# Streamed weights through three buffers, an earlier norm for tile 1, and a ring of gathered rows at a multiple of 8192 bytes

## What is computed

```python
x = x + jnp.concatenate([y_s5, y_m2], axis=-1) @ w_out           # "x_mid" in the kernel
h = rmsnorm(x, norm_ffn_w)
q = (h @ w_q).reshape(T, 8, 2, 128)
s = jnp.einsum('thid,hikd->thik', q, sub_keys)                   # scores
sv, si = lax.top_k(s, 16)                                        # twice, then 16 of 16 x 16
g = jax.nn.softmax(cv, axis=-1)
act = jax.nn.gelu(jnp.einsum('thkd,td->thk', u_tab[idx], h))
x = x + jnp.einsum('thk,thkd->td', g * act, v_tab[idx])          # 128 rows of u and v for each token
y = rmsnorm(x, final_norm_w)
```

## Time and profile before

| what | us |
|---|---|
| median of 3 runs | 4046.57 |
| lowest and highest of them | 4043.29, 4048.2 |
| the profiled execution | 4042.5 |
| its span, first to last instruction | 4040.7 |
| first gather, from the start of the span | 1122.5 |

### The profile page before, as it was taken

The page is one execution under the profiler, slowest core; times in us unless marked ns, Lnnn a source line. Parts: engine busy times, 40 slices in busy tenths (PEclk is TensorE's granted clock), DMA queues, the critical chain, the costliest instruction groups (busy, mean ns, idle before and its releaser), DMA issues.

```text
span 4040.7 us, 47356 instructions
## 1 busy us (share of the span) xinstructions
PE 2634.4 (65%) x16198; PEld 1280.3 (32%) x16198; DVE 2380.2 (59%) x4877; ACT 1190.8 (29%) x2963; POOL 1365.4 (34%) x1291
## 2 busy tenths in 40 slices
PE   7999844978886689764654564564474465455444
PEld 4556733544642233241421231141141141122110
DVE  2355094764556555467577477467567657747744
ACT  2011011114154222233333333333332333333332
POOL 4000010320033444444444444444444444434442
PEclk9999977989998799875755665675585576576555
DMA  3322132457588999998999999999999999999998
GB/s 119 75 71 67 70 40 88 136 178 256 199 314 328 400 421 422 417 417 365 420 421 421 416 421 420 403 420 420 401 420 421 403 418 421 417 404 421 420 413 352
DMA packets 279656, 1318.52 MB, mean 326 GB/s; under 512 B 51632, under 2 KB 111152, under 8 KB 137136
## 3 DMA queue, kind: packets, MB, share of 16 engines
q0 software_dynamic: 156672, 1140.92, 68.4%
q1 hardware_dynamic: 122704, 174.13, 13.4%
HBM read 1266.08 MB, written 46.51 MB: 325 GB/s over the span
## 4 chain that ended last, share of the span: by engine, by line
DMA 45%; issue 12%; PE 9%; DVE 6%; ACT 5%; POOL 1%; POOLq 0%; SPq 0%; DVEq 0%; ACTq 0%
DMA pe_ring<-in_uv,pe_index_now 45%; PE pe_acc L2053 4%; DVE pe_ring L1848 3%; PE pe_ps_q L1916 2%; PE pe_ps_q L1977 2%; ACT pe_mark L1597 1%; ACT L1597 1%; ACT pe_weight L1599 1%; PE pe_ps_t L2046 1%; DMA scratch_s_t<-pe_shared 1%; DVE pe_shared L1655 1%; POOL pe_ring L1475 1%; ACT L1576 0%; PE pe_ps_q L2016 0%; ACT L1559 0%
## 5 line engine op out<-in xcount | busy, mean ns | idle before, releaser
L1848 DVE CUSTOM_DVE_ANT_0 pe_ring<-pe_ring,pe_h_rep 128x1024 f32<-128x1024 f32 x1088 | 1329.2, 1225 | 978.6 <-DMA pe_ring<-in_uv,pe_index_now 927.8
L1475 POOL DMA_INDIRECT pe_ring<-in_uv,pe_index_now x1088 | 1229.0, 1130 | 1575.2 <-PE pe_acc L2053 1407.2
L2053 PE MATMUL pe_acc<-pe_ring,pe_weight 128*32 128x256 f32 x8704 | 980.1, 539 | 1139.4 <-ACT pe_weight L1599 1137.0
L1597 ACT ACTIVATE pe_mark<-pe_same,pe_dot 128x32 f32<-128x32 f32 x1088 | 349.3, 321 | 1782.9 <-DVE pe_dot L1848 1780.3
L2053 PEld LDWEIGHTS pe_acc<-pe_ring,pe_weight 128*32 128x32 f32 x8704 | 205.8, 128 | 1893.5 <-ACT pe_weight L1599 1806.2
L1599 ACT ACTIVATE pe_weight<-pe_mark,pe_gate_now 128x32 f32<-128x32 f32 x1088 | 349.7, 321 | 35.2
L558 PE MATMUL pj_bank<-pj_x_t,pj_w_buf 128*128 128x512 f32 (+1 forms) x960 | 316.0, 491 | 2.7 <-DVE pj_x_t L419 2.7
L2016 PE MATMUL pe_ps_q<-pe_shared,early_space 128*128 128x128 f32 x1792 | 262.5, 307 | 0.0
L2016 PEld LDWEIGHTS pe_ps_q<-pe_shared,early_space 128*128 128x128 f32 x1792 | 239.3, 215 | 47.6 <-issue 47.6
L1977 PE MATMUL pe_ps_q<-early_space,pe_shared 128*128 128x512 f32 x448 | 223.9, 623 | 1.2 <-DVE pe_shared L1655 1.2
L558 PEld LDWEIGHTS pj_bank<-pj_x_t,pj_w_buf 128*128 128x128 f32 x960 | 158.5, 192 | 155.6 <-issue 153.9
(11 more groups left out here) (317 smaller groups left out, 2697.1 us busy)
## 6 DMA issues: line engine op xcount, KB each, us to landing
pe_ring<-in_uv,pe_index_now POOLq DMA_INDIRECT x1088, 16.0
pe_ring<-in_w_out SPq DMA_DIRECT2D x8, 2048.0 KB, 9.0
pe_ring<-in_w_q SPq DMA_DIRECT2D x8, 2048.0 KB, 11.2
pj_w_buf<-in_w_in SPq DMA_DIRECT2D x13, 1024.0 KB, 6.2
early_space<-in_w_out SPq DMA_DIRECT2D x2, 4096.0 KB, 15.9
early_space<-in_w_q SPq DMA_DIRECT2D x8, 1024.0 KB, 47.7
scratch_xbc<-pj_z_out SPq DMA_DIRECT2D x12, 552.0 KB, 4.4
m2s_xbc<-scratch_xbc SPq DMA_DIRECT2D x8, 768.0 KB, 5.1
```

Of the source, the lines that this page charges most:

```text
L1475: nc.gpsimd.indirect_dma_start(out=ring[:, p, :], out_offset=None, in_=D["uv"], in_offset=bass.IndirectOffsetOnAxis(ap=row, axis=0)).then_ ...
L1597: A(mark[:, p % 2, :], eye, ACT.Gelu_apprx_tanh, scale=dot[:, p:p + 1]).then_inc(mark_ready, 1)
L1848: V.tensor_tensor_reduce(out=ring[:, p, 0:D_MODEL], in0=ring[:, p, 0:D_MODEL], in1=h_rep[:, g % 2, :], scale=1.0, scalar=0.0, op0=ALU.mult ...
L2053: last = T.matmul(acc[j * PER:(j + 1) * PER, g % 2, 0:COLS], lhs(j), src[:, j * COLS:(j + 1) * COLS], start=first, stop=final)
```

## The change

1. The pieces go through three buffers: slots 6 and 7, 2 and 3, 4 and 5. `piece_load(i)` waits for piece i - 3. SP issues pieces 0 to 2 at the start, piece 3 ahead of the S5 stores, 4 and 5 between and behind the last gate stores.
2. To make room, the sets of tiles 0 and 1 shrink to one slot each (slots 1 and 0): `res_of` takes the place of `ym_of`, whose transposes have been made by then, and is loaded later; tile 1's S5 tile goes into `h_rep[:, 1]`, once the gate store that reads this buffer has landed.
3. POOL's waits follow the new places: gather 1 (before: 2) waits for `score_moved`; gathers 2, 4 and 6 wait for 6, 7 and 8 query products.
4. `mix(1, X_MID)` stands behind step `SUMS + 2` of `route(0)` instead of `SUMS + 4`, and `route(1, NORM)` behind `SUMS + 4` instead of `SUMS + 6`.
5. Small tensors are allocated ahead of the ring and large ones behind it, so that the ring starts at byte 90,112 of each partition (before: 142,912). With it all tensors allocated behind `pick` move.

```diff
         pick = sb("pick", [P, GROUPS, GROUPS, PER])
+        final_w = sb("final_w", [P, COLS])
+        gate_now = sb("gate_now", [P, SLOTS])
+        mark = sb("mark", [P, 2, PER])
+        count16 = sb("count16", [P, TOPK])
+        norm_w = sb("norm_w", [P, 2 * KT])
+        ring = sb("ring", [P, RING, 2 * D_MODEL])
         ffn_w = sb("ffn_w", [P, D_MODEL])
...
-        piece = [space[:, 8192:12288], space[:, 12288:16384]]
+        piece = [space[:, 4096 * i:4096 * i + 4096] for i in (3, 1, 2)]
...
-        sets = [space[:, 4096:8192], space[:, 0:4096], shared[:, 0:4096], shared[:, 4096:8192]]
+        sets = [space[:, 2048:4096], space[:, 0:2048], shared[:, 0:4096], shared[:, 4096:8192]]
...
-        res_of = lambda m: sets[MIX_SET[m]][:, 1024:2048] if m < EARLY else sets[MIX_SET[m]][:, 3072:4096]
-        m2_of = lambda m: sets[MIX_SET[m]][:, 3072:4096].rearrange("p (c n) -> p c n", c=KT)
+        m2_flat = lambda m: sets[MIX_SET[m]][:, 1024:2048] if m < EARLY else sets[MIX_SET[m]][:, 3072:4096]
+        m2_of = lambda m: m2_flat(m).rearrange("p (c n) -> p c n", c=KT)
+        res_of = lambda m: ym_of(m) if m < EARLY else m2_flat(m)
...
+        s5_tile = lambda m: (h_rep[:, 1, :] if m < EARLY else sets[MIX_SET[m]][:, 2048:3072]).rearrange("p (c n) -> p c n", c=KT)
...
             def piece_load(i):
-                if i >= 2:
-                    sp.wait_ge(*piece_done(i - 2))
+                if i >= 3:
+                    sp.wait_ge(*piece_done(i - 3))
...
-            for i in range(2):
+            for i in range(3):
                 piece_load(i)
-            for m in range(EARLY):
-                sp.dma_start(res_of(m), D["x_all"][rows(m), :]).then_inc(res_in[m], 16)
...
             for m in range(2, TILES):
                 gate_load(m)
+            for m in range(EARLY):
+                sp.wait_ge(m2_turned, m + 1)
+                sp.dma_start(res_of(m), D["x_all"][rows(m), :]).then_inc(res_in[m], 16)
+            piece_load(3)
             sp.wait_ge(s5_ready, KT)
             for b in BLOCK_0:
                 s5_store(0, b, lambda m: s5_1_out if m == 1 else s5_0_out)
-            piece_load(2)
             gate_store(TILES - 2)
-            piece_load(3)
+            piece_load(4)
             gate_store(TILES - 1)
+            piece_load(5)
             sp.wait_ge(s5_1_out, 32)
+            sp.wait_ge(gate_out[1], 16 * (TILES // 2 - 1))
             sp.dma_start(s5_tile(1), D["s5_t"][1]).then_inc(s5_in[1], 16)
-            for i in range(4, 6):
-                piece_load(i)
...
-                    if front and n == 2:
+                    if front and n == 1:
                         pool.wait_ge(score_moved, 1)
-                    if front and n == 4:
-                        pool.wait_ge(q_made, EARLY * UNITS)
+                    if front and n in (2, 4, 6):
+                        pool.wait_ge(q_made, EARLY * UNITS - 3 + n // 2)
...
                 route(0, g, False, 0)
+                if g == SUMS + 2:
+                    mix(1, X_MID)
                 if g == SUMS + 4:
-                    mix(1, X_MID)
-                if g == SUMS + 6:
                     route(1, NORM, True, 1)
```

More of the change, by code:

```diff
@@ L1161, in route_and_experts @@
         pick = sb("pick", [P, GROUPS, GROUPS, PER])
+        final_w = sb("final_w", [P, COLS])
[4 more added lines that the diff above has]
+        ring = sb("ring", [P, RING, 2 * D_MODEL])
         ffn_w = sb("ffn_w", [P, D_MODEL])
-        final_w = sb("final_w", [P, COLS])
-        count16 = sb("count16", [P, TOPK])
         eps = sb("eps", [P, 1])
@@ L1179, in route_and_experts @@
         work_b = shared[:, 6144:8192]
-        norm_w = sb("norm_w", [P, 2 * KT])
         gate_sq = sb("gate_sq", [P, TILES, 2])
@@ L1200, in route_and_experts @@
         gate = e
-        ring = sb("ring", [P, RING, 2 * D_MODEL])
-        mark = sb("mark", [P, 2, PER])
         weight = sb("weight", [P, RING, PER])
@@ L1207, in route_and_experts @@
         h_rep = sb("h_rep", [P, 2, D_MODEL])
-        gate_now = sb("gate_now", [P, SLOTS])
         index_now = sb("index_now", [P, 2, HALF], I32)
@@ L1245, in s5_of @@
         def s5_of(m, c):
-            return s5_out(0, c)[:, first(0):first(0) + P] if m == 0 else sets[MIX_SET[m]][:, 2048 + c * P:2048 + (c + 1) * P]
-        s5_tile = lambda m: sets[MIX_SET[m]][:, 2048:3072].rearrange("p (c n) -> p c n", c=KT)
+            return s5_out(0, c)[:, first(0):first(0) + P] if m == 0 else s5_tile(m)[:, c, :]
+        s5_tile = lambda m: (h_rep[:, 1, :] if m < EARLY else sets[MIX_SET[m]][:, 2048:3072]).rearrange("p (c n) -> p c n", c=KT)
         acc = ctx.enter_context(nc.psum_tensor("pe_acc", [P, 2, 512], F32))
@@ L1269, in route_and_experts @@
         set_3_free = sem("set_3_free")
-        piece_in = [sem("piece_in_even"), sem("piece_in_odd")]
+        piece_in = [sem(f"piece_in{i}") for i in range(3)]
         consts_in, x_in, eps_set, made, summed, root, h_ready = (sem(n) for n in (
@@ L1316, in piece_load @@
             def piece_load(i):
-                if i >= 2:
-                    sp.wait_ge(*piece_done(i - 2))
+                if i >= 3:
+                    sp.wait_ge(*piece_done(i - 3))
                 kind, at = PIECES[i]
                 if kind == "out":
-                    sp.dma_start(out_piece[i % 2], D["w_out"][:, at:at + 4]).then_inc(piece_in[i % 2], 16)
+                    sp.dma_start(out_piece[i % 3], D["w_out"][:, at:at + 4]).then_inc(piece_in[i % 3], 16)
                 else:
-                    sp.dma_start(q_piece[i % 2], D["w_q"][:, :, at * UNIT * P:(at + 1) * UNIT * P]).then_inc(piece_in[i % 2], 16)
+                    sp.dma_start(q_piece[i % 3], D["w_q"][:, :, at * UNIT * P:(at + 1) * UNIT * P]).then_inc(piece_in[i % 3], 16)
             def s5_store(n, b, sem_of):
@@ L1950, in early_out @@
                         pe.wait_ge(s5_ready, KT)
-                pe.wait_ge(piece_in[i % 2], 16 * (i // 2 + 1))
+                pe.wait_ge(piece_in[i % 3], 16 * (i // 3 + 1))
                 for c in range(4 * j % KT, 4 * j % KT + 4):
                     for b in range(2):
-                        last = T.matmul(acc[:, b, :], m2_of(m)[:, c, :] if j < 2 else s5_of(m, c), out_piece[i % 2][:, c % 4, b * 512:b * 512 + 512],
+                        last = T.matmul(acc[:, b, :], m2_of(m)[:, c, :] if j < 2 else s5_of(m, c), out_piece[i % 3][:, c % 4, b * 512:b * 512 + 512],
                                         start=j == 0 and c == 0, stop=j == 3 and c == KT - 1)
@@ L2012, in route @@
                                 i = Q_PIECE[early] + n
-                                pe.wait_ge(piece_in[i % 2], 16 * (i // 2 + 1))
+                                pe.wait_ge(piece_in[i % 3], 16 * (i // 3 + 1))
                         for c in range(KT):
-                            w = w_q[:, c, j * P:(j + 1) * P] if early is None or early == 2 else q_piece[(Q_PIECE[early] + n) % 2][:, c, j % UNIT * P:(j % UNIT + 1) * P]
+                            w = w_q[:, c, j * P:(j + 1) * P] if early is None or early == 2 else q_piece[(Q_PIECE[early] + n) % 3][:, c, j % UNIT * P:(j % UNIT + 1) * P]
                             last = T.matmul(ps_q[:, n % 2, j % UNIT, :], w, h_t[:, c, :],
```

## The result

| | before | after |
|---|---|---|
| median of the runs, us | 4047.39 (4043.29 to 4051.75) | 3988.12 (3983.34 to 3988.76) |
| profiled execution, and its span, us | 4042.5, 4040.7 | 3987.48, 3985.7 |
| the stage's first load to the first gather, us | 894.82 to 1122.47: 227.65 | 898.42 to 1101.29: 202.87 |
| first gather to the end of the span, us | 2918.2 | 2884.4 |
| one tile of 128 gathers, tiles 3 to 6, us | 327.3 to 327.6 | 322.6 to 323.1 |

The ratio is 0.9849, with a 95% interval from 0.983 to 0.9869. A fourth run of the kernel after took 5732.11 us: it is in the median of 3988.12 us, but not in the range and the ratio, and the median of the other three is 3987.48. The third and the fourth row of the table say where the difference lies.

A forecast was written before the change was run, and what follows sets the result against it. PE, waiting for weight loads, was taken to bound the stage ahead of the first gather; 12.77 + 1.11 + 4.33 + 1.70 + 4.70 = 24.6 us off the profiled 4042.5 gave 4017.9, as median 4022.0, range 3996 to 4034.

The forecast's parts named there:

- The first late load: Front, PE's wait for weight piece 2: 11.23 us of wait and 1.54 us of slow clock go, together 12.77.
- The cover of piece 3: Front: piece 3 lands at about 972 us, PE wants it at 975.8; cover 4 us, beyond that each us costs one.
- The other loads: Front, later weight pieces: w_q waits go for 4.33 us, 2.22 shrinks for 1.11, tile 1's wait and clock give 4.70.
- Tile 1's norm: Front, VectorE: with the norm two steps sooner, it ends near 1073.4 instead of 1075.1 us; 1.70 us gained.
- What was costed at nothing in the front: Moved residual loads, SyncE's new waits and the second gather's wait for ScalarE's copy on POOL: hidden, priced at zero.
- The ring's address: Gathered rows landing in the ring, moved from 64 above a multiple of 256 onto one: 0 to 3 ns cheaper, taken as zero.
- the far bound: Upper end of the gain per ring row from the new address: 3 ns.
- rival 1: Gather loop: the ring's new place makes rows 3 ns cheaper, 23 us more gained, 3999 us; chance 0.13.
- everything behind the first gather only moves: Gather loop: same stretch from first gather to end within 8 us, so the front's gain arrives at the end unchanged.
- The 3 ns between the two 4 KB loads: Loads of x_all (aligned, 159.5 ns a row) and x (224 above a multiple, 162.5 ns), used to bound the ring's price.
- The two loads by which the prediction bounded the price: Loads of x_all and x, 4 KB rows at 159.5 and 162.5 ns, bounding an aligned row's gain at 0 to 3 ns.

The follow-up runs named there:

- ring_m64: Changed kernel with one 64-byte tensor moved from ahead of the ring to behind it, ring 192 above a multiple of 256; 4022.47 us.
- ring_m128: Changed kernel with two 64-byte tensors behind the ring instead of ahead, ring 128 above a multiple of 256; 4019.97 us.
- ring_m256: Changed kernel with one 256-byte tensor moved behind the ring, which starts at 89,856, a multiple of 256 but not of 512; 3988.39 us.
- ring_p32: Changed kernel with one 32-byte tensor moved ahead of the ring, ring 32 above a multiple of 256; 4025.23 us.
- ring_back: Changed kernel with the allocation order of the kernel before, ring again 64 above a multiple of 256; 4026.64 us, ratio 0.9942 to the kernel before.
- ring_only: Kernel before with only the allocation order of the changed kernel, ring at byte 90,112; 4013.55 us, ratio 0.992 to the kernel before.
- piece4_first: Changed kernel with the load of piece 4 issued ahead of the six S5 stores; 3988.54 us, ratio 0.9852 to the kernel before.

## Why the prediction was wrong

**The first late load: right.** 11.23 us and 1.54 us were to go. The pair of pieces 2 and 3 starts as the pair before it ends and takes 13.90: 12.77 us. The cover of piece 3 held.

**The other loads: right for w_q, one wait missed.** All brackets of 1.70, 1.01, 1.62 and 3.10 us are gone, and 2.22 became 1.11. What I did not look at is piece 4. I took two pieces of PE's time, 14 us or more, as the cover of every later load, and for that the load has to start as soon as its buffer is free. Piece 4 stands behind the S5 stores on SyncE, and these got slower. Before, PE waited 1.56 us at this place for VectorE:

```profile
997.09 7.10 PE L1954 MATMUL pe_acc<-pe_ring 128*128 128x512 f32 x16 [1.56 <-DVE pe_x L1655]
```

Now it waits 2.30 us for the DMA, and the 16 products behind took 8.72 us instead of 7.10. Cost: 0.74 + 1.62 = 2.4 us. In ring_m64 and ring_m128 the wait is 2.48 us and the products take 7.10 or 7.11, and in ring_m256 and ring_p32 PE waits 1.56 us for VectorE again, so the cost is anything from nothing to 2.4 us. The clock of the kernel after at this place:

```profile
988.30:995.10 6.80, 6.80 (x13) 2.96 (x14) 1.59 (x3) 0.52 (x3) 0.00 (x0) 0.77 1.06 414
```

0.77 is a mixture of the two levels, full speed (2.4 GHz) and half (1.2 GHz), as after the long wait of before (0.79 in the earlier trace rows).

**Tile 1's norm: right.** VectorE's rows of the kernel after answer to the earlier trace rows:

```profile
1054.68 1.22 DVE L1657 TENSOR_TENSOR pe_x<-pe_ring,pe_acc 128x1024 f32<-128x1024 f32 x1 [9.64 <-PE pe_acc L1956]
1055.82 1.64 DVE L1761 MAX8 pe_top<-pe_shared 128x8 f32<-128x256 f32 x4
...
1057.88 1.28 DVE L1719 SCALAR_TENSOR_TENSOR pe_h<-pe_x,pe_stat,pe_ffn_w 128x1024 f32<-128x1024 f32 x1
```

The MAX8 steps stand in between, for 1.64 us (priced at 1.7), and PE's wait falls from 6.48 to 4.64: 1.84 against 1.70. The clock after it is still low, as assumed: 14.96 us for the 112 products, 14.58 before.

**What was costed at nothing in the front: right.** POOL's timeline of the kernel after:

```profile
1101.29 1.16 POOL L1477 DMA_INDIRECT pe_ring<-in_uv,pe_index_now  x1 [0.99 <-POOL pe_index_now L1481]
1103.63 0.94 POOL L1477 DMA_INDIRECT pe_ring<-in_uv,pe_index_now  x1 [1.18 <-ACT pe_shared L1558]
```

and PE's sum of the second gather, in its timeline:

```profile
1115.49 0.64 PE L2055 MATMUL pe_acc<-pe_ring,pe_weight 128*32 128x256 f32 x8
```

The second gather does wait for ScalarE's copy, 1.18 us, and PE uses it 14.2 us after the first one's issue (14.8 forecast). Nobody waits for it. Altogether the front came out at 24.8 us for 24.6, and that it came so near is luck: the fronts of kernels that differ in addresses alone scatter by 3.9 us, and the missed 2.4 us were made up by small parts: the stretch from the turn of tile 0 to the products of tile 1's w_out shrank by 6.1 us instead of 5.4, those products by 0.7, and the stretch behind tile 1's norm by 5.2 instead of 4.7.

**The ring's address: this is the step that failed.** "I take zero, the nearest being the aligned 4 KB row, which per byte is no faster than the ring's rows are now." The bounds were 0 to 3 ns a row; it is 4.6, about half as much again as the far bound, and rival 1 was given 0.13 and 3999 where 3988 came. The rival had the right mechanism and too small a price. With it falls the assumption that everything behind the first gather only moves.

Two things in the trace of before pointed to it. The first is that bytes per ns is the wrong measure between sizes. The packets of the trace of before have these durations:

```
bytes      packets   median ns
 2048 q1     12416         84
 4096 q1     11904        159
 8192 q1       256        309
16384 q1      1312        611
 8192 q0    139264        312   (the ring's rows; mean 316.5 over the whole loop)
```

From 4 KB to 16 KB a packet gains 452 ns for 12,288 bytes, so the line through both gives 159 + 452 / 3 = 310 ns for 8 KB, and the 256 packets of that size that aren't gathers take 309. A 4 KB row is slower per byte because each packet has a fixed part (8 ns on this line). Against that line, which goes through medians, the ring's rows were 2 ns too slow by their median; by their mean in the full queue (314.3 ns) they were 4 to 5, but long packets raise a mean too, so this alone would have left the price open. The 3 ns between the two 4 KB loads, on which the far bound rested, were rounding of the shares: packet by packet these rows took 159.7 and 160.3 ns.

The second is that the ring's own rows were faster at first. Queue of 1132 to 1142 us of the kernel before, and of 1152 to 1162 us:

```profile
q0 software_dynamic: 584, 4.26, 101.5%
...
q0 software_dynamic: 573, 4.17, 100.4%
```

Both are full, and the later one moves 2% less. Packet by packet, with "309" the share of rows that took at most 309 ns:

```
kernel   ring at   stretch, us   rows   mean ns   309    GB/s
before     +64     1132-1142      520    311.3   0.95    426
before     +64     1142-1152      513    312.8   0.24    420
before     +64     1152-1162      509    314.5   0.07    417
before     +64     2600-2700     5101    314.3   0.10    418
ring_back  +64     1111-1121      513    313.6   0.91    420
ring_back  +64     1121-1131      515    313.2   0.41    422
ring_back  +64     1131-1141      512    314.5   0.07    419
ring_m64   +192    1111-1121      518    310.8   0.63    424
ring_m64   +192    1121-1131      513    315.0   0.07    420
after        0     1130-1140      522    309.9   1.00    428
after        0     2600-2700     5172    309.7   1.00    424
```

A row at a start off the multiple takes 309 ns as well while the queue has just filled, and the dearer 312 to 325 only once it has been full for 10 to 20 us. In tile 0 of the kernel before, where other work leaves gaps in the queue (1172 to 1360 us, share 0.89), 83% of the rows are at 309 again. At a multiple of 256 nearly all rows stay at 309 however long the queue is full. So the price is one that only a full queue shows.

The two loads by which the prediction bounded the price could not show it either, because both ran beside ring rows off a multiple. In ring_only the load of x_all from 1574 to 1596 us lands 64 above a multiple, beside ring rows on one, and each of its 128 rows takes 159.0 ns; in before the same load lands on a multiple, beside ring rows off one, and takes 159.7. In ring_m64, where this load and the ring are both off, three loads of x_all take 162.7 to 163.4. So a packet doesn't pay for its own place alone: the place of the rows that fill the queue counts for the other packets too.

The Trainium skill (DMA: Bandwidth & Descriptors, How a descriptor splits into AXI transactions) says that a transaction starts at a multiple of 256 bytes, so that a descriptor of 8 KB that starts elsewhere needs one more. The runs agree that 256 is the multiple that counts, and that 512 and 8192 don't. Its count would make 258 beats instead of 256 for a start at +64, as an estimate 0.8%; measured are 1.5% (314.3 against 309.7 ns), and only under a full queue. It also says that the bytes below the start cost beats, which would make +192 dearer than +32; measured, +32 is the dearest.

**What stays open.** Why a row off the multiple gets dearer only after the queue has been full for a while is not settled: these runs show when it happens, not where in the path, and the split of the price between a row's own place and that of the rows around it was not measured for the ring itself. Whether the reading side, at a table address off a multiple of 256, has the same price was not tried.

## What to carry to other kernels

Where a stage is full of DMA, put the buffer that its rows land in at a multiple of 256 bytes of the partition, by moving small tensors from one side of it to the other; here that was worth 35 us of 4047 and cost nothing. To see from a trace whether rows pay for their place, compare early packets with late ones of the same queue, and packets of one size with the line through other sizes, median with median, and not bytes per ns across sizes. A load that is covered by time must also be issued in time: read what stands ahead of it on its queue, and how much slower that gets when the queue is fuller than before.

## What the runs showed of the hardware that was not expected

- A gathered row of 8 KB takes 309 ns of a DMA engine if it lands at a multiple of 256 bytes, and 313.8 to 315.0 in the mean if it lands 32, 64, 128 or 192 bytes above one, in a queue that stays full. In a queue with gaps most rows take 309 at either place: 83% of them in the kernel before (1172 to 1360 us, share 0.89), 86% in the kernel after (1151 to 1339 us, share 0.88).
- A load of 4 KB rows that landed 64 above a multiple took 159.0 ns a row where the ring's rows lay on a multiple (ring_only), and 162.7 to 163.4 where these lay off one too (ring_m64).
- Issuing the same six stores took SyncE 3.59 and 3.65 us with no large load issued shortly before (before, ring_only), 5.37 to 7.88 in the seven kernels with one load of 2 MB and two of 512 KB ahead of them, and 11.40 with a second load of 2 MB just ahead (piece4_first). So moving a large load up delayed the loads behind the stores. Whether the amount queued or how recently it was queued sets the time is not separated.
